# The router of an expert layer: one-hot matrices from one comparison, a multiplication on GpSimd, and two routes woven on VectorE

## The chip, the cores and the metric

The kernel runs on one core of a Trainium2 chip, in float32. The metric is the device time of one execution in microseconds, the median over several runs. A difference under 0.2% can't be told from run to run variation.

## The reference

One step of a hybrid decoder layer: a modulated norm, one projection, a gated linear attention branch, an RWKV-7 branch, their merge, and then the expert layer (PEER), whose first phase is what changes here:

```python
q = (xt @ peer_wq).reshape(M, 8, 2, 128)
s = einsum('mhpd,hpnd->mhpn', q, peer_keys)          # 2 x 128 scores per token and head
s1, i1 = top_k(s[:, :, 0], 16)
s2, i2 = top_k(s[:, :, 1], 16)
cand = s1[..., :, None] + s2[..., None, :]           # 16 x 16 sums
top, j = top_k(cand.reshape(M, 8, 256), 16)
idx = (i1 * 128 + i2) at j                           # 16 experts of 128 * 128 per token and head
wts = softmax(top)
out = sum over k of gelu(x . u[idx]) * wts * v[idx]
```

There are 1,056 tokens: 1,024 of the prompt in eight tiles of 128, and 32 of the samples.

## The kernel before

The program runs five stages one after the other; the last, the expert layer, has two phases. The second phase (`peer_experts`) takes four tiles of tokens by gathering expert rows, and the other four, the dense tiles, by multiplying with all experts; for these it reads a matrix G from HBM, which has for each token the weight of each of the 128 x 128 experts. The first phase (`peer_routes`) makes the scores of all tokens and G for the four dense tiles. It lies between 2,665 and 3,478 us of the profiled execution.

A route is one head of one tile. TensorE makes a query (16 matrix products) and the scores; ScalarE copies both out of PSUM. For the 32 dense routes VectorE then does the selection (class `Router`): `keys` finds the 16 largest of 128 twice with MAX8, FIND_INDEX8 and MATCH_REPLACE8; `sums` adds them to 16 x 16 candidates and finds the largest 16 of these; `places` looks up their positions by a comparison, a multiplication and a reduction; `weights` finishes the softmax, whose exponentials ScalarE makes (`exps`). Each of these steps needs the one before it, and each waits for it on VectorE's own semaphore (`Chain.link`; `alone` puts a semaphore instruction behind the wait). The scores of the other four tiles and of the samples go to HBM for the second phase.

The loops of all engines run over slots r, one dense route each. When the eight routes of a tile are done, TensorE turns the picks (two positions and a weight for 16 choices of 8 heads) so that the choices lie on the partitions (`picksT`), and in the next eight slots the G of that tile is made, four batches of four tokens per slot (`batches(r)`); the last tile has no routes beside it, and its 32 batches come after the last slot. For each token there are two one-hot matrices of 128 choices x 128 keys: A, in which the first position is marked with the weight, from one VectorE operation per token (L2048), and B, in which the second is marked with one, from ScalarE in two steps, Square of the distance (`far`, L1957) and Relu of one minus it (L1962). TensorE multiplies B with A (L2139), four tokens to a PSUM bank, and ScalarE copies the bank into G in SBUF (L2024). A, B and the bank have two buffers each. When the tile's 32 batches are copied, SyncE stores G, 8 MB in four pieces (L1933); ScalarE waits for that before it copies the next tile's first batch.

The order on each engine is written out by hand. In slot r TensorE does the queries and scores of slot r + 1 (one dense route, one of another tile, and from the 24th slot one of the samples) and then the batches of slot r; ScalarE follows in the same order, with the exponentials between the two; VectorE does the selection of slot r, then its batches, then the weights. GpSimd has nothing to do in this phase.

Of the kernel before, what the change touches and what calls it, by code (L numbers as in the profile page):

```python
# [22 lines left out]
U32 = mybir.dt.uint32  # L23
F32R = mybir.dt.float32r
ALU = mybir.AluOpType
ACT = mybir.ActivationFunctionType
AX = mybir.AxisListType

P = 128
# [47 lines left out]
class Chain:  # L77
# [5 lines left out]
    def link(self, ins):  # L83

        self.n += 1
        ins.then_inc(self.sem, 1)
        self.eng.wait_ge(self.sem, self.base + self.n)

# [1688 lines left out]
class Router:  # L1777
# [68 lines left out]

def peer_routes(nc, t, hT_d):


    with ExitStack() as ctx:  # L1850
# [10 lines left out]
        A, B = s.sb("A", [P, 2, BATCH, KEYS]), s.sb("B", [P, 2, BATCH, KEYS])  # L1861
        far = s.sb("far", [P, 2, BATCH, KEYS])
        G = s.sb("G", [P, KEYS, P])
        r_ = Router(s)
# [3 lines left out]
         ex_ready, picked, p_turned, pT_ready, A_ready, B_ready, g_summed, g_read, g_stored, own, own_act) = (s.sem(n) for n in (  # L1868
             "consts_in wq_in wq_rest_in turned hT_ready q_summed q_ready s_summed s_ready keys_done best_ready "
             "ex_ready picked p_turned pT_ready A_ready B_ready g_summed g_read g_stored own own_act").split())  # L1870
# [13 lines left out]
        def batches(r):  # L1884

            if r < HEADS:
                return range(0)
            if r < ROUTES:
                return range((r - HEADS) * BATCHES // HEADS, (r - HEADS + 1) * BATCHES // HEADS)
            return range((DENSE - 1) * BATCHES, DENSE * BATCHES)  # L1890
# [8 lines left out]
        with nc.Block() as block:  # L1899
            @block.sync  # L1900
            def _(sp):
# [11 lines left out]
                sp.dma_start(r_.iota[:, :], t["iota"].broadcast_to([P, TOP])).then_inc(consts_in, 16)  # L1913
# [3 lines left out]
                for r in range(ROUTES + 1):  # L1917
# [23 lines left out]
            def _(act):  # L1941
                ch = Chain(act, own_act)
                act.wait_ge(consts_in, 16 * 3)
# [8 lines left out]

                def hots(b):

                    for c in range(BATCH):
                        col = b % BATCHES * BATCH + c
                        last = act.activation(far[:, b % 2, c, :], iota[:, :], ACT.Square, scale=-1.0,  # L1957
                                              bias=picksT[:, 1, col:col + 1])
                    ch.link(last)
                    if b >= 2:  # L1960
                        act.wait_ge(g_summed, b - 1)
                    act.activation(B[:, b % 2, :, :], far[:, b % 2, :, :], ACT.Relu, scale=-1.0, bias=1.0).then_inc(B_ready, 1)  # L1962
# [40 lines left out]
                for r in range(ROUTES + 1):  # L2003
# [4 lines left out]
                    if r < ROUTES:  # L2008
                        act.wait_ge(best_ready, r + 1)
                        r_.exps(act).then_inc(ex_ready, 1)  # L2010
                    for b in batches(r):
                        if b % BATCHES == 0:
                            tile = b // BATCHES
                            act.wait_ge(p_turned, tile + 1)
                            act.copy(picksT[:, :, :].rearrange("p a n -> p (a n)"), t_b[:, 0:3 * P]).then_inc(pT_ready, 1)
                            act.wait_ge(pT_ready, tile + 1)
                            hots(b)
                            if tile:
                                act.wait_ge(g_stored, 64 * tile)
                        if (b + 1) % BATCHES:  # L2020
                            hots(b + 1)
# [6 lines left out]
            def _(dve):  # L2028
                ch = Chain(dve, own)
                dve.wait_ge(consts_in, 16 * 3)  # L2030
                for r in range(ROUTES + 1):
                    if r < ROUTES:
                        tile, h = divmod(r, HEADS)
                        cols = slice(h * TOP, (h + 1) * TOP)
                        dve.wait_ge(s_ready, at["dense", r] + 1)
                        r_.keys(dve, ch, sc[:, r % 2, :, :])
                        dve.sem_inc(keys_done, 1)
                        r_.sums(dve, ch).then_inc(best_ready, 1)
                        if h == 0 and tile >= 2:
                            dve.wait_ge(p_turned, tile - 1)  # L2040
                        r_.places(dve, ch, picks[:, tile % 2, 0:2, cols])
                    for b in batches(r):
                        dve.wait_ge(pT_ready, b // BATCHES + 1)
                        if b >= 2:
                            dve.wait_ge(g_summed, b - 1)
                        for c in range(BATCH):
                            col = b % BATCHES * BATCH + c
                            last = dve.tensor_scalar(A[:, b % 2, c, :], iota[:, :], picksT[:, 0, col:col + 1],  # L2048
                                                     picksT[:, 2, col:col + 1], ALU.is_equal, ALU.mult)
                        last.then_inc(A_ready, 1)  # L2050
                    if r < ROUTES:
                        dve.wait_ge(ex_ready, r + 1)
# [3 lines left out]

            @block.tensor
            def _(pe):
                pe.wait_ge(consts_in, 16 * 3)
# [60 lines left out]
                for r in range(ROUTES + 1):  # L2120
# [4 lines left out]
                    for b in batches(r):  # L2125
# [9 lines left out]
                        pe.wait_ge(B_ready, b + 1)  # L2135
                        if b >= 2:
                            pe.wait_ge(g_read, b - 1)
                        for c in range(BATCH):
                            last = pe.matmul(g_b[:, b % 2, c * KEYS:(c + 1) * KEYS], B[:, b % 2, c, :], A[:, b % 2, c, :],  # L2139
# [4 lines left out]
def peer_experts(nc, t, hT_d):  # L2144

    with ExitStack() as ctx:
# [16 lines left out]
        r_ = Router(s)  # L2163
# [495 lines left out]
```

## Time and profile before

| | us |
|---|---|
| median of 3 runs | 5562.33 (5560.19 to 5563.29) |
| the profiled execution | 5564.91 |
| its span, first to last instruction | 5563.0 |

| engine | busy us | share of the span |
|---|---|---|
| TensorE, matmul (PE) | 4561.8 | 82% |
| VectorE (DVE) | 3346.5 | 60% |
| ScalarE (ACT) | 1297.9 | 23% |
| GpSimd (POOL) | 1459.4 | 26% |

The shares are means over the whole program; the phase in question is about a seventh of it and has other shares. Times in the rows are microseconds from the start of the span, durations of single operations are in ns where a row has min/median/max or a mean. A busy PE is not PE at its peak, since matmuls are pipelined and their ends are modelled. Idle time of an engine that does not set the pace costs nothing.

### The profile page before, as it was taken

What the parts mean: (1) busy time and instruction counts of PE and PEld (TensorE: products, weight loads), DVE (VectorE), ACT (ScalarE), POOL (GpSimd) and SP (SyncE); (2) the same over time, 40 slices, a digit from 0 to 9 for tenths busy, and PEclk for the clock granted to TensorE, in tenths of its full rate; (3) what the DMA queues carried; (4) which work ended last, traced back from release to release, by engine and by line L of the source; (5) the groups of instructions that cost most, each with busy time, mean ns of one, the idle gap of its engine ahead of it and who ended that gap; (6) DMA issues with size and microseconds to landing.
All of it is one profiled execution on the core that took longest, in us unless ns stands there. A gap on an engine that the chain in (4) does not pass through costs nothing. (4 is left out here: it accounts for less than half of the span.)

```text
span 5563.0 us, 81870 instructions
## 1 busy us (share of the span) xinstructions
PE 4561.8 (82%) x30972; PEld 3114.4 (56%) x30972; DVE 3346.5 (60%) x7116; ACT 1297.9 (23%) x2733; POOL 1459.4 (26%) x1284
## 2 busy tenths in 40 slices
PE   7999997775777878799676674899999999999980
PEld 1899996554666667564576663344343434434430
DVE  0422332335555555112575552699999999999998
ACT  2100001332333333115155555010110111011001
POOL 0000000000111111000000000557566666656666
PEclk9999998667889888899878885999999999999995
DMA  5222223111000100412202203899999999999998
GB/s 217 87 93 92 92 92 110 56 64 60 28 23 24 34 27 11 174 69 77 105 15 78 69 24 109 347 374 385 353 383 358 380 361 369 385 350 382 360 353 299
DMA packets 354376, 1010.89 MB, mean 182 GB/s; under 512 B 39630, under 2 KB 120462, under 8 KB 349554
## 3 DMA queue, kind: packets, MB, share of 16 engines
q0 software_dynamic: 156672, 570.49, 26.3%
q1 hardware_dynamic: 197372, 435.99, 22.0%
q8 instruction: 206, 3.38, 0.3%
q14 instruction: 126, 1.03, 0.1%
HBM read 902.36 MB, written 103.99 MB: 181 GB/s over the span
## 5 line engine op out<-in xcount | busy, mean ns | idle before, releaser
L2509 PE MATMUL peer_v_b<-peer_vt,peer_mix 128*128 128x512 f32 x2048 | 944.4, 616 | 127.0 <-DVE peer_mix L2346 80.6
L2276 POOL DMA_INDIRECT peer_ring<-in_peer_u,peer_idx x544 | 596.4, 1096 | 1692.5 <-DVE peer_idx L2383 1266.6
L2497 PE MATMUL peer_s_b<-dense_hT_d,peer_ut 128*128 128x512 f32 x2048 | 901.3, 593 | 51.3 <-DMA peer_G2s<-mod 51.3
L2282 POOL DMA_INDIRECT peer_ring<-in_peer_v,peer_idx x544 | 715.4, 1315 | 293.0 <-issue 160.3
L2509 PEld LDWEIGHTS peer_v_b<-peer_vt,peer_mix 128*128 128x128 f32 x2048 | 402.5, 198 | 652.9 <-issue 498.5
L2497 PEld LDWEIGHTS peer_s_b<-dense_hT_d,peer_ut 128*128 128x128 f32 x2048 | 389.8, 190 | 542.2 <-issue 490.6
L2398 DVE SCALAR_TENSOR_TENSOR peer_acc<-peer_ring,peer_coef,peer_acc 128x1024 f32<-128x1024 f32 x534 | 653.9, 1280 | 0.0
L2435 DVE CUSTOM_DVE_ANT_0 peer_ring<-peer_ring,peer_h 128x1024 f32<-128x1024 f32 x544 | 637.5, 1220 | 2.0 <-DVE peer_h L2412 1.0
L1357 POOL TENSOR_TENSOR rw_An<-rw_abT,rw_join 128x256 f32<-128x256 f32 x160 | 126.0, 794 | 1924.8 <-DVE rw_abT L1267 1542.5
L56 PE MATMUL proj_acc<-proj_hT_high,proj_w_low 128*128 128x352 f32 x1584 | 512.2, 323 | 25.8 <-DVEq L353 25.8
L57 PE MATMUL proj_acc<-proj_hT_low,proj_w_high 128*128 128x352 f32 x1584 | 508.6, 321 | 0.0
L58 PE MATMUL proj_acc<-proj_hT_high,proj_w_high 128*128 128x352 f32 x1584 | 508.2, 321 | 0.0
L2139 PE MATMUL route_g_b<-route_A,route_B 128*128 128x128 f32 x1024 | 203.5, 362 | 208.9 <-DVE route_A L2048 78.4
L49 DVE TENSOR_SCALAR proj_masked<-proj_w 128x1024 uint32<-128x1024 uint32 x66 | 45.8, 694 | 495.8 <-PE proj_acc L58 491.4
L56 PEld LDWEIGHTS proj_acc<-proj_hT_high,proj_w_low 128*128 128x128 f32 x1584 | 298.0, 188 | 26.5 <-issue 23.5
L2139 PEld LDWEIGHTS route_g_b<-route_A,route_B 128*128 128x128 f32 x1024 | 178.1, 262 | 231.2 <-DVE route_A L2048 119.0
L57 PEld LDWEIGHTS proj_acc<-proj_hT_low,proj_w_high 128*128 128x128 f32 x1584 | 298.5, 188 | 0.0
L58 PEld LDWEIGHTS proj_acc<-proj_hT_high,proj_w_high 128*128 128x128 f32 x1584 | 297.6, 188 | 0.0
L2048 DVE TENSOR_SCALAR route_A<-route_iota,route_picksT 128x128 f32<-128x128 f32 x512 | 140.6, 342 | 233.0 <-PE route_g_b L2139 194.9
L1625 PE MATMUL mg_acc<-mg_br,mg_w 128*128 128x352 f32 x768 | 229.0, 461 | 20.7 <-DMA mg_br<-ogT 20.7
L1301 DVE TENSOR_TENSOR rw_T<-rw_T,rw_t_b 128x256 f32<-128x256 f32 x256 | 106.2, 419 | 203.6 <-PE rw_t_b L1473 201.7
L2294 ACT ACTIVATE peer_gelu<-peer_s_b 128x512 f32<-128x512 f32 x128 | 74.8, 593 | 599.3 <-PE peer_s_b L2497 598.9
(418 smaller groups left out, 7015.3 us busy)
## 6 DMA issues: line engine op xcount, KB each, us to landing
peer_ut<-in_peer_ut SPq DMA_DIRECT2D x128, 512.0 KB, 9.9
peer_vt<-in_peer_v SPq DMA_DIRECT2D x128, 512.0 KB, 7.9
pT<-proj_o SPq DMA_DIRECT2D x66, 528.0 KB, 3.0
proj_w<-in_w_in SPq DMA_DIRECT2D x66, 512.0 KB, 4.2
G<-route_G SPq DMA_DIRECT2D x16, 2048.0 KB, 16.6
peer_gt<-G SPq DMA_DIRECT2D x128, 256.0 KB, 5.9
mod_w<-in_w_ada SPq DMA_DIRECT2D x12, 2048.0 KB, 8.2
peer_ring<-in_peer_u,peer_idx POOLq DMA_INDIRECT x544, 10.2
```

The lines of the kernel that those rows point to most:

```text
L56: pe.matmul(out, w[1], x[0], start=start, stop=False)
L57: pe.matmul(out, w[0], x[1], start=False, stop=False)
L58: return pe.matmul(out, w[0], x[0], start=False, stop=stop)
L1625: last = pe.matmul(acc[b][:, g, 0:G3], w[:, n, b, k, :], br[:, b, k, g * G3:(g + 1) * G3], start=(k == 0), stop=(k == KD - 1))
L2048: last = dve.tensor_scalar(A[:, b % 2, c, :], iota[:, :], picksT[:, 0, col:col + 1], picksT[:, 2, col:col + 1], ALU.is_equal, ALU.mult)
L2139: last = pe.matmul(g_b[:, b % 2, c * KEYS:(c + 1) * KEYS], B[:, b % 2, c, :], A[:, b % 2, c, :], start=True, stop=True)
L2276: pool.indirect_dma_start(out=ring[:, k, :], out_offset=None, in_=t["peer_u"], in_offset=bass.IndirectOffsetOnAxis(ap=idx[U % 2][:, k:k + ...
L2282: pool.indirect_dma_start(out=ring[:, k, :], out_offset=None, in_=t["peer_v"], in_offset=bass.IndirectOffsetOnAxis(ap=idx[U % 2][:, k:k + ...
L2398: dve.scalar_tensor_tensor(out=to, in0=ring[:, k, :], scalar=coef[:, k:k + 1], in1=to, op0=ALU.mult, op1=ALU.add).then_inc(v_used, 1)
L2435: dve.tensor_tensor_reduce(ring[:, k, :], ring[:, k, :], h[:, tile % 2, :], 1.0, 0.0, ALU.mult, ALU.add, dots[:, k:k + 1]).then_inc(u_used, 1)
L2497: last = pe.matmul(s_b[:, n % 3, :], ut[:, n % UT, k, :], hT_d[:, k, :], start=(k == 0), stop=(k == KD - 1))
L2509: last = pe.matmul(v_b[:, m % 4, :], mix[:, part % 2, e, tokens], vt[:, part % 2, e, cols], start=(e == 0), stop=(e == PART - 1))
```

## The change

Both one-hot matrices of a batch come from one VectorE comparison over [2, 4, 128] elements of a partition, into one tile AB with three buffers. GpSimd multiplies the A half by the weights, in place. ScalarE's Square and Relu are gone. The selection is written as two streams of steps, `keys` of route r and `pairs` of route r - 1, and `weave` issues them in turn on VectorE, each with a wait for the step that it needs; `top` and `pos` have two buffers for that. The batches begin one slot later, and there is one slot more. The second phase keeps the former class under the name `OldRouter`.

```diff
+    def mark(self, ins):
+
+        self.n += 1
+        ins.then_inc(self.sem, 1)
+        return self.n
+
+    def need(self, n):
+
+        self.eng.wait_ge(self.sem, self.base + n)
...
-class Router:
+class OldRouter:
...
+class Router:
+
+    def __init__(self, s, iota):
+        self.iota = iota
+        self.top, self.pos = s.sb("top", [P, 2, 2, TOP]), s.sb("pos", [P, 2, 2, TOP], U32)
+        self.posf = s.sb("posf", [P, 2, TOP])
+        self.cand = s.sb("cand", [P, TOP, TOP])
+        self.best, self.j16, self.j2 = s.sb("best", [P, TOP]), s.sb("j16", [P, TOP], U32), s.sb("j2", [P, 2, TOP], U32)
+        self.jf = s.sb("jf", [P, 2, TOP])
+        self.hot = s.sb("hot", [P, 2, TOP, TOP])
+        self.sel = s.sb("sel", [P, 2, TOP])
+        self.ex, self.z = s.sb("ex", [P, TOP]), s.sb("z", [P, 2])
+        self.passed = s.sem("passed")
+
+    def after(self, dve, ch, n):
+
+        if n is not None:
+            ch.need(n)
+        dve.sem_inc(self.passed, 1)
+
+    def top16(self, dve, ch, n, vals, val, place):
+
+        for half in range(2):
+            o8 = slice(8 * half, 8 * half + 8)
+            self.after(dve, ch, n)
+            n = ch.mark(dve.max(val[:, o8], vals))
+            yield n
+            self.after(dve, ch, n)
+            n = ch.mark(dve.max_index(place[:, o8], val[:, o8], vals))
+            yield n
+            if half == 0:
+                self.after(dve, ch, n)
+                n = ch.mark(dve.match_replace(vals, val[:, o8], vals, LOWEST))
+                yield n
+
+    def keys(self, dve, ch, c, sc, keys_done):
+
+        n = None
+        for half in range(2):
+            for n in self.top16(dve, ch, n, sc[:, half, :], self.top[:, c % 2, half, :], self.pos[:, c % 2, half, :]):
+                yield
+        ch.need(n)
+        dve.sem_inc(keys_done, 1)
+        yield
+
+    def pairs(self, dve, ch, c, best_ready):
+
+        top, pos = self.top[:, c % 2, :, :], self.pos[:, c % 2, :, :]
+        dve.tensor_copy(self.posf[:, :, :], pos)
+        n = ch.mark(dve.tensor_tensor(self.cand[:, :, :], top[:, 0, :].unsqueeze(2).broadcast_to([P, TOP, TOP]),
+                                      top[:, 1, :].unsqueeze(1).broadcast_to([P, TOP, TOP]), ALU.add))
+        yield
+        for n in self.top16(dve, ch, n, self.cand[:, :, :].rearrange("p a b -> p (a b)"), self.best, self.j16):
+            yield
+        ch.need(n)
+        dve.tensor_scalar(self.z[:, 1:2], self.best[:, 0:1], -1.0, None, ALU.mult).then_inc(best_ready, 1)
+        dve.tensor_scalar(self.j2[:, 0, :], self.j16[:, :], 4, None, ALU.logical_shift_right)
+        n = ch.mark(dve.tensor_scalar(self.j2[:, 1, :], self.j16[:, :], TOP - 1, None, ALU.bitwise_and))
+        yield
+        ch.need(n)
+        n = ch.mark(dve.tensor_copy(self.jf[:, :, :], self.j2[:, :, :]))
+        yield
+        ch.need(n)
+        n = ch.mark(dve.tensor_tensor(self.hot[:, :, :, :], self.jf[:, :, :].unsqueeze(3).broadcast_to([P, 2, TOP, TOP]),
+                                      self.iota[:, 0:TOP].unsqueeze(1).unsqueeze(1).broadcast_to([P, 2, TOP, TOP]), ALU.is_equal))
+        yield
+        ch.need(n)
+        n = ch.mark(dve.tensor_tensor(self.hot[:, :, :, :], self.hot[:, :, :, :],
+                                      self.posf[:, :, :].unsqueeze(2).broadcast_to([P, 2, TOP, TOP]), ALU.mult))
+        yield
+        ch.need(n)
+        n = ch.mark(dve.tensor_reduce(self.sel[:, :, :], self.hot[:, :, :, :], AX.X, ALU.add))
+        yield
+        ch.need(n)
+
+    def exps(self, act):
+
+        return act.activation(self.ex[:, :], self.best[:, :], ACT.Exp, bias=self.z[:, 1:2], accum_out=self.z[:, 0:1])
+
+    def weights(self, dve, ch, to):
+
+        ch.link(dve.reciprocal(self.z[:, 0:1], self.z[:, 0:1]))
+        ch.link(dve.tensor_scalar(to, self.ex[:, :], self.z[:, 0:1], None, ALU.mult))
+
+def weave(*streams):
+
+    streams = list(streams)
+    while streams:
+        for x in list(streams):
+            if next(x, streams) is streams:
+                streams.remove(x)
...
-        A, B = s.sb("A", [P, 2, BATCH, KEYS]), s.sb("B", [P, 2, BATCH, KEYS])
-        far = s.sb("far", [P, 2, BATCH, KEYS])
+        AB = s.sb("AB", [P, 3, 2, BATCH, KEYS])
         G = s.sb("G", [P, KEYS, P])
-        r_ = Router(s)
+        r_ = Router(s, iota)
...
-            if r < HEADS:
+            if r <= HEADS:
                 return range(0)
-            if r < ROUTES:
-                return range((r - HEADS) * BATCHES // HEADS, (r - HEADS + 1) * BATCHES // HEADS)
+            if r <= ROUTES:
+                return range((r - HEADS - 1) * BATCHES // HEADS, (r - HEADS) * BATCHES // HEADS)
...
-                sp.dma_start(r_.iota[:, :], t["iota"].broadcast_to([P, TOP])).then_inc(consts_in, 16)
...
-                for r in range(ROUTES + 1):
+                for r in range(ROUTES + 2):
...
-                ch = Chain(act, own_act)
-                act.wait_ge(consts_in, 16 * 3)
+                act.wait_ge(consts_in, 16 * 2)
...
-                def hots(b):
-
-                    for c in range(BATCH):
-                        col = b % BATCHES * BATCH + c
-                        last = act.activation(far[:, b % 2, c, :], iota[:, :], ACT.Square, scale=-1.0,
-                                              bias=picksT[:, 1, col:col + 1])
-                    ch.link(last)
-                    if b >= 2:
-                        act.wait_ge(g_summed, b - 1)
-                    act.activation(B[:, b % 2, :, :], far[:, b % 2, :, :], ACT.Relu, scale=-1.0, bias=1.0).then_inc(B_ready, 1)
...
-                    if r < ROUTES:
-                        act.wait_ge(best_ready, r + 1)
+                    if 0 < r <= ROUTES:
+                        act.wait_ge(best_ready, r)
...
-                            act.wait_ge(pT_ready, tile + 1)
-                            hots(b)
                             if tile:
                                 act.wait_ge(g_stored, 64 * tile)
-                        if (b + 1) % BATCHES:
-                            hots(b + 1)
...
-                for r in range(ROUTES + 1):
+                dve.wait_ge(consts_in, 16 * 2)
+                for r in range(ROUTES + 2):
+                    streams = []
                     if r < ROUTES:
-                        tile, h = divmod(r, HEADS)
+                        dve.wait_ge(s_ready, at["dense", r] + 1)
+                        streams.append(r_.keys(dve, ch, r, sc[:, r % 2, :, :], keys_done))
+                    if 0 < r <= ROUTES:
+                        tile, h = divmod(r - 1, HEADS)
                         cols = slice(h * TOP, (h + 1) * TOP)
-                        dve.wait_ge(s_ready, at["dense", r] + 1)
-                        r_.keys(dve, ch, sc[:, r % 2, :, :])
-                        dve.sem_inc(keys_done, 1)
-                        r_.sums(dve, ch).then_inc(best_ready, 1)
+                        streams.append(r_.pairs(dve, ch, r - 1, best_ready))
+                    weave(*streams)
+                    if 0 < r <= ROUTES:
                         if h == 0 and tile >= 2:
                             dve.wait_ge(p_turned, tile - 1)
-                        r_.places(dve, ch, picks[:, tile % 2, 0:2, cols])
+                        ch.link(dve.tensor_copy(picks[:, tile % 2, 0:2, cols], r_.sel[:, :, :]))
                     for b in batches(r):
                         dve.wait_ge(pT_ready, b // BATCHES + 1)
-                        if b >= 2:
-                            dve.wait_ge(g_summed, b - 1)
-                        for c in range(BATCH):
-                            col = b % BATCHES * BATCH + c
-                            last = dve.tensor_scalar(A[:, b % 2, c, :], iota[:, :], picksT[:, 0, col:col + 1],
-                                                     picksT[:, 2, col:col + 1], ALU.is_equal, ALU.mult)
-                        last.then_inc(A_ready, 1)
-                    if r < ROUTES:
-                        dve.wait_ge(ex_ready, r + 1)
+                        if b >= 3:
+                            dve.wait_ge(g_summed, b - 2)
+                        cells = slice(b % BATCHES * BATCH, (b % BATCHES + 1) * BATCH)
+                        dve.tensor_tensor(AB[:, b % 3, :, :, :],
+                                          iota[:, :].unsqueeze(1).unsqueeze(1).broadcast_to([P, 2, BATCH, KEYS]),
+                                          picksT[:, 0:2, cells].unsqueeze(3).broadcast_to([P, 2, BATCH, KEYS]),
+                                          ALU.is_equal).then_inc(hot_ready, 1)
+                    if 0 < r <= ROUTES:
+                        dve.wait_ge(ex_ready, r)
                         r_.weights(dve, ch, picks[:, tile % 2, 2, cols])
                         if h == HEADS - 1:
                             dve.sem_inc(picked, 1)
 
+            @block.gpsimd
+            def _(pool):
+                for b in range(DENSE * BATCHES):
+                    pool.wait_ge(hot_ready, b + 1)
+                    pool.wait_ge(pT_ready, b // BATCHES + 1)
+                    cells = slice(b % BATCHES * BATCH, (b % BATCHES + 1) * BATCH)
+                    pool.tensor_tensor(AB[:, b % 3, 0, :, :], AB[:, b % 3, 0, :, :],
+                                       picksT[:, 2, cells].unsqueeze(2).broadcast_to([P, BATCH, KEYS]),
+                                       ALU.mult).then_inc(A_ready, 1)
...
-                        pe.wait_ge(B_ready, b + 1)
...
-                            last = pe.matmul(g_b[:, b % 2, c * KEYS:(c + 1) * KEYS], B[:, b % 2, c, :], A[:, b % 2, c, :],
+                            last = pe.matmul(g_b[:, b % 2, c * KEYS:(c + 1) * KEYS], AB[:, b % 3, 1, c, :], AB[:, b % 3, 0, c, :],
```

## Rows read from the trace of the kernel before

**Rows 1.** Windows: length, busy us of PE, PEld, DVE, ACT, POOL, PEclk, DMA, GB/s

```profile
2695.40:2788.40 93.00, 77.26 (x649) 76.40 (x650) 73.14 (x295) 16.41 (x55) 0.00 (x0) 0.94 0.08 25
2788.40:2941.80 153.40, 111.93 (x780) 107.25 (x779) 107.74 (x424) 96.22 (x235) 0.00 (x0) 0.81 0.05 14
2941.80:2984.10 42.30, 17.23 (x110) 16.46 (x111) 13.52 (x55) 14.10 (x33) 0.00 (x0) 0.65 0.75 214
2984.10:3118.30 134.20, 102.09 (x787) 97.50 (x786) 94.26 (x372) 89.40 (x218) 0.00 (x0) 0.92 0.05 16
3118.30:3163.80 45.50, 21.04 (x143) 20.35 (x143) 13.47 (x54) 14.25 (x35) 0.00 (x0) 0.67 0.68 194
3163.80:3324.50 160.70, 122.48 (x876) 118.96 (x876) 94.33 (x372) 89.31 (x219) 0.00 (x0) 0.83 0.04 12
3324.50:3446.00 121.50, 69.32 (x275) 60.29 (x275) 36.03 (x131) 89.45 (x202) 0.00 (x0) 0.51 0.25 70
```

**Rows 2.** Waits from 2679 to 3466: total us, times, longest us

```profile
DVE route_A L2048 <- PE route_g_b L2139: 194.9, 78, 29.2
```

**Rows 3.** Timeline of VectorE, one early route: start us, us, instruction

```profile
2707.41 0.29 DVE L1800 MAX8 route_top<-route_sc 128x8 f32<-128x128 f32 x1 [0.18 <-DVE route_picks L1844]
2707.86 0.09 DVE L1801 MATCH_VALUE_LOAD route_pos<-route_top,route_sc 128x8 f32 x1
...
2709.38 0.28 DVE L1801 FIND_INDEX8 route_pos<-route_top,route_sc 128x8 uint32<-128x128 f32 x1
2709.58 0.28 DVE L1800 MAX8 route_top<-route_sc 128x8 f32<-128x128 f32 x1
...
2717.73 0.69 DVE L1835 TENSOR_REDUCE route_picks<-route_hot 128x32 f32<-128x512 f32 x1
...
2719.07 0.30 DVE L1800 MAX8 route_top<-route_sc 128x8 f32<-128x128 f32 x1 [0.18 <-DVE route_picks L1844]
```

**Rows 4.** Timeline of all engines around the last tile's batches

```profile
3330.74 20.64 SPq L1933 DMA_DIRECT2D G<-route_G  x4
...
3361.39 1.28 ACT L1957 ACTIVATE route_far<-route_iota,route_picksT 128x128 f32<-128x128 f32 x4 [28.38 <-DMA G<-route_G]
...
3402.65 1.12 DVE L2048 TENSOR_SCALAR route_A<-route_iota,route_picksT 128x128 f32<-128x128 f32 x4 [1.52 <-PE route_g_b L2139]
...
3403.76 1.26 ACT L1957 ACTIVATE route_far<-route_iota,route_picksT 128x128 f32<-128x128 f32 x4
3405.06 0.63 ACT L1962 ACTIVATE route_B<-route_far 128x512 f32<-128x512 f32 x1
...
3405.59 1.03 ACT L2024 COPY route_G<-route_g_b 128x512 f32<-128x512 f32 x1
...
3405.78 2.04 PE L2139 MATMUL route_g_b<-route_A,route_B 128*128 128x128 f32 x8 [0.60 <-issue]
```

**Rows 5.** Timeline of TensorE in a slot with three queries

```profile
3192.40 5.73 PE L2090 MATMUL route_q_b<-dense_hT_d,route_wq 128*128 128x128 f32 x32
...
3198.41 3.74 PE L2090 MATMUL route_q_b<-route_hT_g,route_wq 128*128 128x128 f32 x32
```

**Rows 6.** Groups of VectorE instructions by line, recurrent stage: busy us, mean ns

```profile
L1195 DVE TENSOR_TENSOR rw_shifted<-rw_Ed 128x1023 f32<-128x1023 f32 x8 | 9.7, 1213 | 0.0
```

**Rows 7.** Timeline in the recurrent stage, GpSimd beside VectorE

```profile
1392.09 1.31 DVE L1203 SCALAR_TENSOR_TENSOR rw_rkv<-rw_shifted,rw_cst,rw_Ed 128x1056 f32<-128x1056 f32 x1
...
1392.85 1.13 POOL L1357 TENSOR_TENSOR rw_An<-rw_abT,rw_join 128x256 f32<-128x256 f32 x1 [3.64 <-PE rw_t_b L1460]
...
1400.57 0.85 POOL L1357 TENSOR_TENSOR rw_An<-rw_abT,rw_join 128x256 f32<-128x256 f32 x1 [6.59 <-PE rw_t_b L1460]
...
1400.87 1.67 DVE L1240 SCALAR_TENSOR_TENSOR rw_km<-rw_rkv,rw_cst 128x1056 f32<-128x1056 f32 x1
...
1405.60 0.73 POOL L1357 TENSOR_TENSOR rw_An<-rw_abT,rw_join 128x256 f32<-128x256 f32 x1 [4.18 <-PE rw_t_b L1460]
```

**Rows 8.** One line of GpSimd: duration in ns, min/median/max

```profile
L1373 POOL TENSOR_TENSOR rw_bk_seq<-rw_nat_smp,rw_seq_rows x16: 1041/1043/1225, 1427.5 to 2240.8; 128x512 f32<-128x512 f32 x16
```

More of the change, by code:

```diff
@@ L1867, in peer_routes @@
         (consts_in, wq_in, wq_rest_in, turned, hT_ready, q_summed, q_ready, s_summed, s_ready, keys_done, best_ready,
-         ex_ready, picked, p_turned, pT_ready, A_ready, B_ready, g_summed, g_read, g_stored, own, own_act) = (s.sem(n) for n in (
+         ex_ready, picked, p_turned, pT_ready, hot_ready, A_ready, g_summed, g_read, g_stored, own) = (s.sem(n) for n in (
              "consts_in wq_in wq_rest_in turned hT_ready q_summed q_ready s_summed s_ready keys_done best_ready "
-             "ex_ready picked p_turned pT_ready A_ready B_ready g_summed g_read g_stored own own_act").split())
+             "ex_ready picked p_turned pT_ready hot_ready A_ready g_summed g_read g_stored own").split())
         h_in, sc_stored = [s.sem(f"h_in{n}") for n in range(2)], [s.sem(f"sc_stored{n}") for n in range(2)]
@@ L2029, in _ @@
                 ch = Chain(dve, own)
-                dve.wait_ge(consts_in, 16 * 3)
-                for r in range(ROUTES + 1):
+                dve.wait_ge(consts_in, 16 * 2)
+                for r in range(ROUTES + 2):
+                    streams = []
                     if r < ROUTES:
-                        tile, h = divmod(r, HEADS)
+                        dve.wait_ge(s_ready, at["dense", r] + 1)
+                        streams.append(r_.keys(dve, ch, r, sc[:, r % 2, :, :], keys_done))
+                    if 0 < r <= ROUTES:
+                        tile, h = divmod(r - 1, HEADS)
@@ L2055, in _ @@
                             dve.sem_inc(picked, 1)
+            @block.gpsimd
[7 more added lines that the diff above has]
+                                       ALU.mult).then_inc(A_ready, 1)
             @block.tensor
             def _(pe):
-                pe.wait_ge(consts_in, 16 * 3)
+                pe.wait_ge(consts_in, 16 * 2)
                 def turn(tile):
@@ L2119, in _ @@
                 routes(0)
-                for r in range(ROUTES + 1):
+                for r in range(ROUTES + 2):
                     if r + 1 < ROUTES:
@@ L2162, in peer_experts @@
         ss, eps = s.sb("ss", [P, 1 + DENSE]), s.sb("eps", [P, 1])
-        r_ = Router(s)
+        r_ = OldRouter(s)
         UT = 3
```

## The prediction

> **What bounds the kernel now.** I read first the busy time of each engine by stage [rows 1]. The seven windows are cut at DVE's instructions: the first eight routes (93.0 us), eight slots with four batches each (153.4), the slot in which the second tile's first batch comes (42.3), seven slots (134.2), the same slot for the third tile (45.5), seven more (160.7), and the fourth tile's 32 batches alone (121.5). No engine is full in any of them: DVE 73 of 93 us in the first, PE 112 and DVE 108 of 153 in the second, ACT 89 of 121.5 in the last. So the phase is bound by handing over, and the order of each engine's program says by whom.
>
> In the first window DVE has no wait on another engine, yet stands still for a fifth of the time. The DVE rows [rows 3] show why: one route takes 11.66 us from its first MAX8 to that of the next; a dependent step starts 0.16 us after the end of the one before it, whereas the MAX8 that begins the second half, which waits for nothing, starts 0.08 us before the end of FIND_INDEX8. In the last window ACT is a closed loop: Square 1.26, Relu 0.63, copy of G 1.03 [rows 4], one batch each 2.65 us (84.6 us for the 32 after the stall); PE's 2.04 us lies inside it. The waits name the same loop from DVE's side: 194.9 us of DVE waiting in these windows for the matmuls of G, which wait for ACT's matrix [rows 2]. In the slots between, PE goes through the next slot's queries and then through four batches at ACT's pace: 9.9 us of batches plus some 9.5 us of queries and scores make 19.2, and with the sample routes (three queries, 5.73 + 3.74 + 3.74 us and the scores, some 14 us [rows 5]) 24. At the changes of tile ACT waits for the store of G: 28.38 us in the last case, in which the store is issued at 3330.74 and ACT goes on at 3361.39 [rows 4].
>
> **The change, part by part.**
>
> *ACT's part of the one-hot matrix is removed*: 5 instructions per batch, 1.89 us. ACT keeps 1.03 per batch and 2 us per slot of other copies, so it limits nothing any more.
>
> *DVE's comparison.* Four operations, 1.12 us together [rows 4], become one of 1,024 elements. The nearest row is the 128x1023 tensor_tensor, 1.213 us [rows 6]; I take 1.22 and see no reason for another end, since shape, type and engine are the same. DVE saves nothing here.
>
> *GpSimd's multiplication, a new step between comparison and matmul.* The nearest row is GpSimd's 128x512 multiplication with two broadcast operands, 1.043 us in the median and 1.225 at most [rows 8]; I take 1.04. By itself it would hide behind DVE. It does not: in the recurrent stage a GpSimd multiplication of 128x256 takes 0.73 alone, but 1.13 when it starts inside a DVE operation with two SBUF inputs, and a DVE operation of 1.31 takes 1.67 when it starts inside one on GpSimd [rows 7]. The two are done one after the other: 1392.09 to 1393.98 is 1.89 us, for 1.31 + 0.73 = 2.04 alone. So a pair of comparison and multiplication costs between 1.22 + 1.04 - 0.15 - 0.2 = 1.9 and their sum, 2.26; I take 2.15. This is the Trainium skill's "SBUF — State Buffer", section "Who interferes with whom": a Vector instruction with two SBUF inputs and a GpSimd instruction that reads SBUF exclude each other for a whole instruction; by its "fully blocks", with a hand-over of about 115 ns as the page's "bandwidth-pool" section gives, the pair would be 2.38, the tail 7 us longer. The rows show 0.15 less than full exclusion, and I go by them.
>
> Batches are thus 2.15 us apart in the tail where they were 2.65, although DVE, GpSimd and ACT each need 1.0 to 1.2. PE's batch of 2.04 still fits below.
>
> *In a slot*: the first comparison starts, the second follows it at once, GpSimd gets the SBUF after that, then they alternate. The fourth comparison needs the slot's first matmuls (three buffers) and ends some 6.2 us after the first began; weights 0.45; the multiplications that are left hold up `cand` in the weave, 0.4. That is 7.1 us of DVE per slot.
>
> *The weave.* Unwoven, keys and pairs take 2707.41 to 2718.42, 11.0 us [rows 3]. At best all the idle time goes and each step starts 0.08 before the end of its predecessor: a fifth of 11.66 is 2.4 us, and about 15 new overlaps give 1.1, so 7.5; at worst nothing changes and the copy into picks adds 0.2, so 11.2. Every step still carries its wait and the semaphore instruction, but the result that it needs was finished while the other route's step ran, and those run 0.2 to 0.4 us, more than the 0.16. I take 8.2, near the lower end; weights stay 0.45.
>
> *One more slot.* Slot 0 has only keys (4.5 us), slot 32 only pairs, and the batches start a slot later. All DMAs of the routes keep their place; SP loses one 8 KB load. G's stores still follow the 32nd copy, with the sample scores behind them on SP's queue.
>
> **The sum**, in own time of the profiled execution:
> Slots 0 to 8: 4.5, then PE limits rather than DVE: 77.3 us of work for eight slots [rows 1], less what it runs ahead, about 9.2 each against DVE's 8.7. 78 for 93.0: -15.
> Slots 9 to 16: DVE 8.2 + 0.45 counted above + 7.1 = 15.5 to 16; PE's 112 / 8 = 14.0 fits. 8 x 16 = 128 for 153.4: -25.
> Slot 17: the stall stays, but DVE can do the next weave in it. 33 for 42.3: -9.
> Slots 18 to 24: 5 x 16 + 23 (two turns) + 18.7 = 122 for 134.2: -12.
> Slot 25: sample scores wait behind the store, ACT with them. 42 for 45.5: -3.5.
> Slots 26 to 32: PE sets the pace: 14 us of queries, then four batches that lie ready, 4.7: 18.7. 5 x 18.7 + 16 + 14 = 123.5 for 160.7: -37.
> Tail: 4.3 to the last copy of the third tile, store 30.6, two batches at once, 30 x 2.15 = 64.5: 101.5 for 121.5: -20.
> Together -122. The profiled execution took 5564.9 (span 5563.0), 2.6 above the median of the runs: 5562.3 - 122 = 5440.
>
> **The rivals.**
>
> *The weave gives nothing* (keys and pairs 11.2). For it: each step keeps its wait and its semaphore instruction. Against it: the independent pair in [rows 3]. Then slots 1 to 8 take 11.8, the slots with batches 18.7, those with three queries 19.5: +6, -4, -7, +3, -1, -30, -20, together -53: 5510. The Trainium skill's "VectorE: DVE Perf Modes", section "The DRAIN you can't avoid", would have it so: the next operation waits for the pipeline of the one before to empty, with or without semaphores. The trace disagrees: MAX8 at 2709.58 starts before FIND_INDEX8 ends at 2709.66.
>
> *GpSimd and DVE do not hold each other up*, the operands being broadcasts. For it: nothing but that no row has this pair of shapes. Then the slots fall to PE's 14.0, those with three queries to 17, the tail to 1.9 per batch: -15, -41, -11, -26, -4, -50, -28: 5387.
>
> *GpSimd's step is dearer and the phase slower than before*: its place is between each comparison and the matmuls. The gain of 122 over 128 batches is 0.96 us per batch; from a multiplication of 2.0 us on the change loses. At twice the held-up 128x256 row (2 x 1.13 = 2.26, 1.22 above mine) it would be +156 - 122 = +34: 5596. For it: operand and output are the same tile, which no GpSimd row here has; against it: the 128x512 row with like broadcasts.
>
> **Chances.** Forecast 0.66 (5405 to 5475 by the bounds of weave and pair), weave without gain 0.17, no mutual hold-up 0.10, dearer GpSimd 0.05, none of these with no visible change 0.02. The range 5390 to 5515 holds the forecast, most of the second and a part of the third. A change under 0.2% (11 us) can't be told from none here. Faster 0.93, same 0.02, slower 0.05.
>
> **What the profile after would show.** DVE comparisons of about 1.2 us that alternate with GpSimd operations, some of them at 1.8 to 2.2 because they were held; batches 2.1 to 2.3 apart in the tail; ACT without Square and Relu; DVE over 85% busy in the slots without batches, routes there under 9.5 us apart. Wrong would be: gaps of 0.15 us between woven steps (second case), comparisons that overlap multiplications at full speed (third), GpSimd operations of over 2 us with no DVE operation beside them (fourth). If PE's granted clock fell to the lower level through the slots, PE and not DVE would set them and the sum would be too good.

## The result and the profile after

| | before | after |
|---|---|---|
| median of the runs compared, us | 5561.26 (4 runs) | 5422.72 (4 runs, 5420.07 to 5427.57) |
| the profiled execution | 5564.91 | 5427.57 |
| its span | 5563.0 | 5425.8 |

The ratio is 0.9758 with a 95% interval of 0.9743 to 0.9774: 138.5 us faster, where 122 had been forecast; 5422.72 lies inside the range and inside the likeliest case's own bounds.

First, where the time went. The windows below are cut like those of before [rows 1], at VectorE's instructions: from the first MAX8 to the weights of the eighth route, eight slots, the next eight with the stall at the change of tile, the slot with the second stall, the seven slots with three queries, and the last tile from there to its store.

```profile
2702.60:2780.29 77.69, 75.48 (x674) 75.25 (x674) 64.66 (x303) 17.94 (x56) 0.00 (x0) 1.00 0.11 37
2780.29:2904.38 124.09, 103.74 (x824) 99.49 (x823) 116.46 (x321) 46.66 (x82) 51.44 (x31) 0.94 0.04 14
2904.38:3057.09 152.71, 118.13 (x938) 113.50 (x936) 115.46 (x322) 52.10 (x92) 50.65 (x33) 0.88 0.25 74
3057.09:3100.32 43.23, 18.60 (x144) 17.97 (x145) 14.56 (x41) 6.79 (x13) 5.97 (x4) 0.73 0.71 204
3100.32:3214.91 114.59, 93.49 (x770) 90.63 (x770) 97.47 (x265) 42.20 (x73) 41.81 (x28) 0.92 0.04 14
3214.91:3309.94 95.03, 48.13 (x276) 42.51 (x275) 54.55 (x35) 35.94 (x36) 55.83 (x33) 0.74 0.31 89
```

| stage | before | forecast | measured |
|---|---|---|---|
| slots 0 to 8 | 93.0 | 78 | 77.7 |
| 9 to 16 | 153.4 | 128 | 124.1 |
| 17 to 24 (42.3 + 134.2) | 176.5 | 155 | 152.7 |
| 25 | 45.5 | 42 | 43.2 |
| 26 to 32 | 160.7 | 123.5 | 114.6 |
| the last tile | 121.5 | 101.5 | 95.0 |
| together | 750.6 | 628 | 607.3 |

The six stages account for 143.3 us; in this execution the stages ahead of the phase, whose code is the same, took some 7 us longer (the first window begins at 2702.60, before at 2695.40) and what follows it 1 us less, which leaves the 137.2 between the spans. Each window shows which engine is near its full time: TensorE in the first (75.5 of 77.7 us), VectorE in the second (116.5 of 124.1, where before it had 107.7 of 153.4 and TensorE 111.9). A part of VectorE's busy time is waiting inside its instructions (below; 104.4 us in experiment 3, where that is gone). ScalarE went from 96 us to 47 there.

The weave, in VectorE's timeline of a slot without batches (start, duration, instruction):

```profile
2721.42 0.29 DVE L1886 MAX8 route_top<-route_sc 128x8 f32<-128x128 f32 x1 [0.18 <-DVE route_picks L1943]
...
2722.11 0.28 DVE L1889 FIND_INDEX8 route_pos<-route_top,route_sc 128x8 uint32<-128x128 f32 x1
2722.31 0.41 DVE L1886 MAX8 route_best<-route_cand 128x8 f32<-128x256 f32 x1
...
2728.00 0.69 DVE L1932 TENSOR_REDUCE route_sel<-route_hot 128x32 f32<-128x512 f32 x1
2728.72 0.18 DVE L2134 COPY route_picks<-route_sel 128x32 f32<-128x32 f32 x1
2728.93 0.16 DVE L1942 RECIPROCAL route_z<-route_z 128x1 f32<-128x1 f32 x1
```

MAX8 on the candidates of one route starts at 2722.31, 0.08 before FIND_INDEX8 of the other route ends at 2722.39: nearly each step of the weave does what only the independent pair did before [rows 3]. Keys and pairs with the copy take 2721.42 to 2728.90, 7.5 us, the lower of the two bounds.

The pair of comparison and multiplication, first by line (ns, min/median/max), then in the last tile's timeline:

```profile
L2140 DVE TENSOR_TENSOR route_AB<-route_iota,route_picksT x128: 1211/1226/2075, 2788.7 to 3303.7; 128x1024 f32<-128x1024 f32 x128
L2156 POOL TENSOR_TENSOR route_AB<-route_AB,route_picksT x128: 1035/1954/2096, 2790.0 to 3306.6; 128x512 f32<-128x512 f32 x128
```

```profile
3249.46 1.88 ACT L2114 COPY route_G<-route_g_b 128x512 f32<-128x512 f32 x2 [30.33 <-DMA G<-route_G]
...
3256.28 11.88 POOL L2156 TENSOR_TENSOR route_AB<-route_AB,route_picksT 128x512 f32<-128x512 f32 x6 [1.16 <-DVE route_AB L2140]
...
3259.55 1.74 DVE L2140 TENSOR_TENSOR route_AB<-route_iota,route_picksT 128x1024 f32<-128x1024 f32 x1 [0.24 <-PE route_g_b L2241]
3260.27 1.16 PE L2241 MATMUL route_g_b<-route_AB 128*128 128x128 f32 x8 [0.82 <-POOL route_AB L2156]
3261.46 1.03 ACT L2114 COPY route_G<-route_g_b 128x512 f32<-128x512 f32 x1 [0.94 <-PE route_g_b L2241]
3261.53 1.74 DVE L2140 TENSOR_TENSOR route_AB<-route_iota,route_picksT 128x1024 f32<-128x1024 f32 x1 [0.24 <-PE route_g_b L2241]
```

The shortest duration of each is its own (1.21, 1.04); what the others have beyond that is read here as waiting inside the instruction for the other engine, which experiment 3 tests: six multiplications stand end to end for 11.88 us, 1.98 each, and comparisons of 1.74 start 1.98 apart. Of 1.22 + 1.04 = 2.26 only 0.28 is saved.

### The profile page after: what moved, and what is told of

It is laid out like the page before. It is cut to its first block and busy times, and to the rows that moved or that the text cites. A ratio compares the mean times of both kernels' runs of the same rounds, so it can differ in the third digit from the quotient of the medians.

```text
span 5425.8 us, 80977 instructions
## 1 busy us (share of the span) xinstructions
PE 4506.1 (83%) x30972; PEld 3060.4 (56%) x30972; DVE 3376.8 (62%) x6700; ACT 1090.8 (20%) x2093; POOL 1667.9 (31%) x1412
## 5 line engine op out<-in xcount | busy, mean ns | idle before, releaser
L2156 POOL TENSOR_TENSOR route_AB<-route_AB,route_picksT 128x512 f32<-128x512 f32 x128 | 205.7, 1631 | 852.0 <-DVE route_AB L2140 852.0
L2241 PE MATMUL route_g_b<-route_AB 128*128 128x128 f32 x1024 | 167.6, 323 | 143.0 <-POOL route_AB L2156 97.5
L2140 DVE TENSOR_TENSOR route_AB<-route_iota,route_picksT 128x1024 f32<-128x1024 f32 x128 | 195.4, 1562 | 116.7 <-PE route_g_b L2241 80.3
L2241 PEld LDWEIGHTS route_g_b<-route_AB 128*128 128x128 f32 x1024 | 149.3, 227 | 160.1 <-POOL route_AB L2156 114.0
```

Of the source, the lines that this page charges most:

```text
L2156: pool.tensor_tensor(AB[:, b % 3, 0, :, :], AB[:, b % 3, 0, :, :], picksT[:, 2, cells].unsqueeze(2).broadcast_to([P, BATCH, KEYS]), ALU.mu ...
L2241: last = pe.matmul(g_b[:, b % 2, c * KEYS:(c + 1) * KEYS], AB[:, b % 3, 1, c, :], AB[:, b % 3, 0, c, :], start=True, stop=True)
```

## Experiments

Each was run with the kernel before on the same chip: its median was 5558.95 us beside the first four and 5556.87 beside the last two (7 runs each). Kernels run beside different runs of the kernel before are compared by their ratios, of a time of 5560 us: the change itself is 134.5 us by its ratio. As a second measure, the phase in the one profiled execution of each, from the first MAX8 to the store of the last tile's G, took 750.2 us before, 607.3 in the changed kernel, and 704.4, 713.4, 561.6, 700.5, 595.9 and 548.4 in experiments 1 to 6. What each saves by the one measure and by the other agrees within 10 us. The code ahead of the phase, the same in all, took from 2681.7 to 2708.4 us, so the time of one execution can move by that much without the change.

**1. No weave.** Same steps, same waits, but the streams of a slot one after the other:

```diff
-                    weave(*streams)
+                    for x in streams:
+                        weave(x)
```

> The changed kernel with the two streams issued one after the other (first all steps of keys, then all of pairs); slots, buffers and one-hot matrices as changed. Theory (each dependent step stands still 0.15 us behind its predecessor, and the weave fills that): keys and pairs take 11.0 to 11.4 us per route instead of 7.5; +3.7 on 8 slots without batches (30 us), +3.7 on 14 with two queries (52), +2.5 to 3 on 8 with three (22): 5423 + 100 = 5525, between 5500 and 5540. Rival (TensorE sets the slots, VectorE's steps are hidden): under +35, 5425 to 5458.

Measured: 5513.99 us, ratio 0.9919 (0.9902 to 0.9936). This lies in the theory's range. The price of 5510 given to the prediction's second case is close to what a kernel without the gain takes, in part by luck: slots 0 to 16 are some 17 us dearer than that case had them, the last tile 6.5 cheaper. The windows of its first eight routes and of slots 9 to 16, then the first and the last steps of keys and pairs in one slot:

```profile
2690.76:2797.65 106.89, 88.92 (x736) 87.84 (x736) 77.62 (x302) 18.16 (x60) 0.00 (x0) 0.94 0.09 30
2797.65:2955.88 158.23, 107.88 (x764) 103.58 (x765) 128.60 (x321) 44.86 (x78) 47.64 (x31) 0.80 0.03 10
```

```profile
2738.01 0.30 DVE L1886 MAX8 route_top<-route_sc 128x8 f32<-128x128 f32 x1 [0.18 <-DVE route_picks L1943]
2738.45 0.09 DVE L1889 MATCH_VALUE_LOAD route_pos<-route_top,route_sc 128x8 f32 x1
...
2747.71 0.69 DVE L1928 TENSOR_TENSOR route_hot<-route_hot,route_posf 128x512 f32<-128x512 f32 x1
2748.44 0.69 DVE L1932 TENSOR_REDUCE route_sel<-route_hot 128x32 f32<-128x512 f32 x1
2749.16 0.18 DVE L2135 COPY route_picks<-route_sel 128x32 f32<-128x32 f32 x1
```

The first eight routes' 300 instructions of VectorE take 77.6 us of busy time in 106.9, where woven they take 64.7 in 77.7. Keys and pairs with the copy take 11.3 us where woven they take 7.5, and a slot with batches takes 19.8 us instead of 15.5. Without the weave the change is worth 45 us by the ratio; the weave brings the other 90, once the batches are in their new form. The rows also show that not every dependent step stands still as long: those with a semaphore instruction behind their wait start 0.14 to 0.15 after the end of the one before (MATCH_VALUE_LOAD at 2738.45 after 2738.31), those with the wait alone 0.03 to 0.04 (the reduction at 2748.44 after 2748.40). So most of the idle time that the weave fills goes with that instruction; what unwoven streams without it would take was not run.

**2. Weave alone.** The old matrices, A by four VectorE operations and B by ScalarE's Square and Relu, with the woven selection.

```diff
-                        dve.tensor_tensor(AB[:, b % 3, :, :, :], ..., ALU.is_equal).then_inc(hot_ready, 1)
+                        for c in range(BATCH):
+                            col = b % BATCHES * BATCH + c
+                            last = dve.tensor_scalar(A[:, b % 2, c, :], iota[:, :], picksT[:, 0, col:col + 1],
+                                                     picksT[:, 2, col:col + 1], ALU.is_equal, ALU.mult)
+                        last.then_inc(A_ready, 1)
...
```

> The changed kernel with the former one-hot matrices: A from four VectorE operations per batch, B from ScalarE's Square and Relu, two buffers each, no GpSimd; the weave and the shifted slots stay. Theory (the loop of ScalarE's 2.65 us per batch and TensorE's queries sets the slots with batches): those stay at 19.2 and 24 us and the tail at 2.65 per batch; only the slots without batches gain 15 to 18, the additional slot costs about 10: 5545 to 5565. Rival (the two halves of the change add up): the gain of the weave alone is what its removal costs, some 100: 5450 to 5475.

Measured: 5522.44 us, ratio 0.9936 (0.9919 to 0.9952), between the two expectations; neither held. The windows of slots 0 to 8, 9 to 16, 17 to 24 and 26 to 32:

```profile
2690.81:2768.57 77.76, 75.47 (x673) 75.24 (x674) 64.69 (x302) 17.94 (x56) 0.00 (x0) 1.00 0.12 37
2768.57:2913.66 145.09, 110.61 (x828) 106.02 (x826) 96.11 (x416) 97.00 (x237) 0.00 (x0) 0.88 0.04 12
2913.66:3098.58 184.92, 125.70 (x931) 120.62 (x931) 95.94 (x417) 104.45 (x252) 0.00 (x0) 0.83 0.21 61
...
3144.19:3283.05 138.86, 104.94 (x768) 100.64 (x768) 82.15 (x349) 87.53 (x214) 0.00 (x0) 0.84 0.03 11
```

Before the batches come the weave brings all it brings in the changed kernel (77.8 us for 93.0). With them it brings 8 us in eight slots, loses 8 in the next eight (184.9 for 176.5) and brings 22 in slots 26 to 32 (138.9 for 160.7): as the batches begin a slot later, one slot with three queries more falls to the eight, and one fewer to the seven. The waits say why the slots with batches gain so little:

```profile
DVE route_A L2158 <- PE route_g_b L2249: 255.4, 78, 28.9
```

VectorE's wait for the matmuls of G, which hang on ScalarE's matrix, was 194.9 us [rows 2] and is 255.4: most of the time that the weave frees goes into it. The theory's number was too high since the extra slot costs little: the ninth slot has no batches (8.1 us), and the last two of the phase have no queries. The halves alone are worth 36 us (this one) and 45 (the one before), 81 together, and the change 134.5: each alone runs into the limit that the other removes.

**3. No contention.** The comparison reads the positions where TensorE's transposes left them, in PSUM, and not ScalarE's copy in SBUF; so it has one SBUF input instead of two. GpSimd is as it was.

```diff
-                                          picksT[:, 0:2, cells].unsqueeze(3)...
+                                          t_b[:, 0:2 * P].rearrange("p (a n) -> p a n", a=2)[:, :, cells].unsqueeze(3)...
```

> The changed kernel in which the comparison reads the turned picks from PSUM, where TensorE put them, instead of ScalarE's copy in SBUF; GpSimd still reads the copy. So the comparison has one SBUF input. Theory (two SBUF inputs of VectorE and a GpSimd operation exclude each other): comparisons 1.2 us and multiplications 1.04 throughout, overlapping; batches in the tail 1.2 to 1.4 apart while TensorE is at the high clock, up to 1.9 where it is not, for 1.98; slots with batches 13 to 14 for 15.35; 5365 to 5400. Rival (1.95 us is the price of this GpSimd operation itself, in place and with a broadcast operand): nothing changes, 5415 to 5430.

Measured: 5370.45 us (5360.88 to 5379.01), ratio 0.9666 (0.965 to 0.9682), faster than the changed kernel and in the theory's range. By line:

```profile
L2140 DVE TENSOR_TENSOR route_AB<-route_iota,route_t_b x128: 1212/1220/1223, 2768.9 to 3238.7; 128x1024 f32<-128x1024 f32 x128
L2156 POOL TENSOR_TENSOR route_AB<-route_AB,route_picksT x128: 1038/1039/1042, 2770.2 to 3240.0; 128x512 f32<-128x512 f32 x128
```

Every comparison takes 1.21 to 1.22 and every multiplication 1.04, in the same program order and with the same buffers. In the last tile the two run side by side:

```profile
3224.08 15.86 DVE L2140 TENSOR_TENSOR route_AB<-route_iota,route_t_b 128x1024 f32<-128x1024 f32 x13
3224.24 2.17 POOL L2156 TENSOR_TENSOR route_AB<-route_AB,route_picksT 128x512 f32<-128x512 f32 x2 [0.22 <-DVE route_AB L2140]
```

13 comparisons in 15.86 us, 1.22 each where they were 1.98 apart. So the hold-up of the pair cost some 51 us (0.9758 less 0.9666; 46 by the phase), and its place is the comparison's second SBUF input. The third case of the prediction (no hold-up, 5387) was wrong for the kernel as changed and about right for this one. The Trainium skill's "SBUF — State Buffer", section "Who interferes with whom", states this: a Vector instruction with at most one SBUF input, outside the modes that use both ports, does not contend with GpSimd. The trace agrees for these shapes.

**4. GpSimd's step doubled.** One more GpSimd multiplication per batch (the B half by itself, ones and zeros):

```diff
+                    pool.tensor_tensor(AB[:, b % 3, 1, :, :], AB[:, b % 3, 1, :, :], AB[:, b % 3, 1, :, :], ALU.mult)
```

> The changed kernel with one more GpSimd operation per batch, the B half (zeros and ones) multiplied by itself into itself, 512 elements like the first. Theory (mutual exclusion): each costs about 1.0 us per batch on the path: batches in the tail 3.0 apart (+30 us), slots with batches 3 to 4 us longer (+70 to +90): 5510 to 5545, most of the gain lost, as the forecast's point of decision (a multiplication dearer by 0.96 us) says. Rival (GpSimd runs beside VectorE and only its own 2.1 us per batch count): +3 to +12, 5425 to 5440.

Measured: 5517.53 us, ratio 0.9921 (0.9904 to 0.9937). By the ratios it is 91 us above the changed kernel, 0.71 us per batch for 1.04 of GpSimd where the theory had about 1.0, so most of GpSimd's time is on the path and the time is in the theory's range. Not all of it need be the hold-up: TensorE waits more here and its granted clock is lower too, 0.87 in slots 9 to 16 where it was 0.94, and no run separates the two. The window of these slots, 144.8 us instead of 124.1, and VectorE's comparisons, held:

```profile
2787.14:2931.89 144.75, 114.04 (x828) 108.58 (x826) 117.03 (x321) 46.67 (x82) 83.90 (x61) 0.87 0.04 12
```

```profile
L2140 DVE TENSOR_TENSOR route_AB<-route_iota,route_picksT x128: 1217/1690/2065, 2795.5 to 3400.0; 128x1024 f32<-128x1024 f32 x128
```

If further time cost the same, an estimate, the gain would be gone at 1.04 x 134.5 / 91 = 1.5 us more per batch; the prediction's break-even was 0.96, since it took every microsecond as lying on the path and the gain as 122.

**5. The multiplication on VectorE.** GpSimd does nothing in the phase; each comparison is followed by a 128x512 multiplication on VectorE itself:

```diff
+                        dve.wait_ge(hot_ready, b + 1)
+                        dve.tensor_tensor(AB[:, b % 3, 0, :, :], AB[:, b % 3, 0, :, :],
+                                          picksT[:, 2, cells].unsqueeze(2).broadcast_to([P, BATCH, KEYS]),
+                                          ALU.mult).then_inc(A_ready, 1)
...
```

> The multiplication by the weights is a second VectorE operation of 128x512 behind each comparison; GpSimd does nothing in this phase. Theory (comparison and multiplication exclude each other, so GpSimd's step takes VectorE's time almost whole): a batch costs 1.22 plus half of that, 0.61, plus the gaps of a dependent pair, 1.85 to 2.0 us of VectorE for the 1.98 of the changed kernel; the time stays within 20 us of 5423, 5403 to 5440, and the weights' 128x16 operation falls back from 0.77 to about 0.24 us, since nothing holds it. Rival (GpSimd carries a real part of the batch beside VectorE): 0.5 us and more per batch come on top, 5470 to 5490.

Measured: 5407.16 us, ratio 0.9739 (0.9715 to 0.9763), at or a little below the changed kernel's 0.9758, as the theory had it: the intervals overlap, the phase is 11 us shorter. The timeline in the last tile:

```profile
3234.35 1.22 DVE L2140 TENSOR_TENSOR route_AB<-route_iota,route_picksT 128x1024 f32<-128x1024 f32 x1
3235.60 0.69 DVE L2145 TENSOR_TENSOR route_AB<-route_AB,route_picksT 128x512 f32<-128x512 f32 x1
3236.21 1.22 DVE L2140 TENSOR_TENSOR route_AB<-route_iota,route_picksT 128x1024 f32<-128x1024 f32 x1
```

A batch is 1.86 us of VectorE alone; with GpSimd it was 1.98. The second engine brought nothing here: what VectorE would do in 0.64 it is held for 0.76.

**6. Five buffers**, on top of experiment 3: AB has five in place of three, and the comparison waits for the matmuls of five batches earlier.

```diff
-        AB = s.sb("AB", [P, 3, 2, BATCH, KEYS])
+        AB = s.sb("AB", [P, 5, 2, BATCH, KEYS])
...
-                            dve.wait_ge(g_summed, b - 2)
+                            dve.wait_ge(g_summed, b - 4)
...
```

> The comparison reads picks from PSUM, as in the kernel that read them there with three buffers (5370), and the pair of matrices has five buffers in place of three, so that VectorE can run four batches ahead of the matmuls. Theory (with the hold-up gone TensorE and VectorE are each about 0.9 busy in a slot and run nearly level; a buffer can only take out what one waits for the other): 0 to 15 us less, 5355 to 5370. Rival (the wait for a free buffer, 82 us in that trace, is a real limit of the slots): 40 us less and more, 5330 or below.

Measured: 5357.02 us, ratio 0.9644 (0.962 to 0.9669), the fastest of all and in the theory's range. The interval overlaps that of experiment 3, so a gain over it is not certain; the phase, 13 us shorter, agrees with one, and so do the windows (slots 9 to 16 here, and there):

```profile
2772.85:2880.22 107.37, 99.14 (x828) 95.38 (x826) 103.42 (x320) 46.69 (x82) 32.21 (x31) 0.98 0.05 16
```

```profile
2760.49:2872.07 111.58, 100.71 (x828) 95.73 (x827) 104.35 (x320) 47.28 (x83) 32.22 (x31) 0.98 0.05 15
```

TensorE and VectorE now fill 92% and 96% of a slot, so both would have to be relieved for much more.

## Why the prediction was right

*Direction and mechanism* held: ScalarE's loop was the limit, its removal put the limit on VectorE and, where there are three queries, on TensorE. Experiments 1 and 2 show that both halves are needed for that. What the third buffer of AB brings by itself was not measured. Two of the signs named ahead came out differently: batches are 1.98 apart in the last tile (2.1 to 2.3 had been named), and VectorE is 83% busy in the slots without batches (over 85%), since TensorE sets these.

*The weave* was mis-sized: 8.2 us taken, 7.5 measured. The 0.7 is 5.6 us over slots 9 to 16; the wait and the semaphore instruction cost next to nothing once another step lies between. The reading that a dependent step starts 0.16 us behind the one before holds for the steps with that instruction only (experiment 1). In slots 0 to 8 it makes no difference, since TensorE sets them, as forecast (78 and 77.7). As to the second case, the Trainium skill's "VectorE: DVE Perf Modes", section "The DRAIN you can't avoid", says too that a next operation that is not held starts earlier, so read whole it does not speak for that case.

*The pair* was mis-sized: 2.15 taken, 1.98 measured, between the bounds of 1.9 and 2.26. The 0.2 in the lower bound stands there without a row. The estimate of 2.38 from the hand-over of 115 ns, given for a DMA's descriptors in the Trainium skill's "SBUF — State Buffer", section "A bandwidth-pool intuition that's wrong (but worth ruling out)", is not borne out: the rows show less than the sum, not more. In the last tile, 60.5 us lie between ScalarE's return at 3249.46 and the store at 3309.94, where 64.5 and the first two batches were forecast: most of the 6.5 us there.

*VectorE's batches in a slot* were sized right: the four comparisons of a slot take from 2804.77 to 2811.00, 6.2 us as forecast. The weights behind them were taken as unchanged at 0.45 with their gaps, and are dearer (below), which gives a part of the weave's 5.6 back.

*The slots with three queries* were the largest error: 18.7 taken, 16.6 measured, and 9 us over slots 26 to 32. The failed step is "14 us of queries", read from a slot in which the first query took 5.73 us and the others 3.74 [rows 5]. TensorE in such a slot of the changed kernel:

```profile
3135.89 3.74 PE L2193 MATMUL route_q_b<-dense_hT_d,route_wq 128*128 128x128 f32 x32
...
3139.91 3.74 PE L2193 MATMUL route_q_b<-route_hT_g,route_wq 128*128 128x128 f32 x32
...
3143.93 3.74 PE L2193 MATMUL route_q_b<-route_hT_s,route_wq 128*128 128x128 f32 x32
```

All three take 3.74. Windows of the kernel before, over the 5.73 us query of [rows 5], the one behind it, and the batches ahead of them:

```profile
3182.40:3192.40 10.00, 5.21 (x34) 4.73 (x34) 5.64 (x26) 9.83 (x26) 0.00 (x0) 0.87 0.04 15
3192.40:3198.10 5.70, 5.70 (x35) 5.70 (x35) 4.69 (x19) 1.58 (x3) 0.00 (x0) 0.63 0.00 0
3198.41:3202.10 3.69, 3.69 (x36) 3.69 (x35) 2.83 (x9) 0.50 (x2) 0.00 (x0) 1.00 0.11 36
```

ScalarE is busy 9.83 of the 10 us of the batches and TensorE 5.21; then the first query has a granted clock of 0.63 and the next of 1.00, so the first ran mostly at the lower of TensorE's two levels (1.2 and 2.4 GHz). In the changed kernel, where the batches lie ready and TensorE waits 0.4 us among them in a slot, its clock is 0.92 over the stage (0.83 before), and the first query is as fast as the others. Three of 3.74 with their scores are 12.1 us, 2 less than taken. So less waiting came back a second time as a faster TensorE. The other runs point the same way: in slots 26 to 32 all these first queries take 3.74 in experiment 1, which waits about half as long between batches as the kernel before, and three of five take 4.6 to 5.1 in experiment 2, which has the old batches; no run changed the clock alone. The prediction had named only the opposite, a falling clock, as a danger.

*The stalls* behind the store of G stay about as forecast (30.33 us at 3249.46, 28.38 before), and slot 25 with them (43.2 us for 42); at the first change of tile slots 17 and 18 take 52.8 us, 4 more than forecast.

## What to carry to other kernels

Two halves of a change that lift different limits of one loop can't be added up from trials of each alone: 36 and 45 us here made 134.5. An operation moved to GpSimd was free here only once VectorE's operation beside it had a single SBUF input; look for an operand that already lies in PSUM before moving work, since that was worth some 50 us here and the move by itself nothing. Where the engine that is about to become the limit ran partly at its lower clock while it was waiting between steps, work out the sum from rows at the upper level as well.

## What was not expected of the hardware

Two small operations of VectorE with a single tensor input are held up by GpSimd too. The weights' 128x16 operation (one tensor and a scalar per partition) took 0.235 us before. In the changed kernel, in experiment 3, and in experiment 5, in this order (ns, min/median/max):

```profile
L1943 DVE TENSOR_SCALAR route_picks<-route_ex,route_z x32: 234/820/1043, 2721.0 to 3215.1; 128x16 f32<-128x16 f32 x32
```

```profile
L1943 DVE TENSOR_SCALAR route_picks<-route_ex,route_z x32: 233/1039/1042, 2701.2 to 3168.5; 128x16 f32<-128x16 f32 x32
```

```profile
L1943 DVE TENSOR_SCALAR route_picks<-route_ex,route_z x32: 233/234/236, 2709.8 to 3196.4; 128x16 f32<-128x16 f32 x32
```

With GpSimd idle it is 0.234 in all 32; in experiment 3 its median is that of a whole GpSimd operation, and the one at 2843.36 starts 0.03 after such an operation at 2843.33 and lasts as long:

```profile
2843.33 1.04 POOL L2156 TENSOR_TENSOR route_AB<-route_AB,route_picksT 128x512 f32<-128x512 f32 x1 [0.36 <-DVE route_AB L2140]
```

```profile
2843.36 1.04 DVE L1943 TENSOR_SCALAR route_picks<-route_ex,route_z 128x16 f32<-128x16 f32 x1
```

The cast of 128x32 that opens the pairs shows the same (0.62 us at 2812.39 for 0.16 at 2721.63). So a small operation with one input can cost 0.8 us when it comes right behind the last batch; what it would bring to move it away from there was not measured. The statement cited at experiment 3 leaves out the modes that use both ports; whether these two operations ran in one, no trace here shows.
